# First block's opening: modulation products with the condition as the stationary operand on four column groups

## The reference, cut to what matters

```
c_act = jax.nn.silu(c)
for l in range(DEPTH):
    mod = c_act @ w_ada[l] + b_ada[l]                 # 1024 x 3072 weights
    shift, scale, gate = jnp.split(mod, 3, axis=-1)
    h = rms_norm(x, norm_g[l]) * (1.0 + scale[:, None]) + shift[:, None]
    proj = h @ w_in[l]
    ...
```

## Time and profile before

| | us |
|---|---|
| median of 3 runs | 2635.62 |
| lowest and highest | 2634.14, 3508.53 |
| the profiled execution: its time | 2632.88 |
| its span in the profile | 2631.1 |
| PE busy in the span | 2471.4 (94%) |
| DVE, ACT, POOL busy | 1205.1, 983.9, 631.0 |
| first product of the second stage | 94.13 after the span's start |

### The profile page before, as it was taken

The page is one execution under the profiler, slowest core; times in us unless marked ns, Lnnn a source line. Parts: engine busy times, 40 slices in busy tenths (PEclk is TensorE's granted clock), DMA queues, the critical chain, the costliest instruction groups (busy, mean ns, idle before and its releaser), DMA issues. The chain is left out here.

```text
span 2631.1 us, 33028 instructions
## 1 busy us (share of the span) xinstructions
PE 2471.4 (94%) x13180; PEld 2023.3 (77%) x13180; DVE 1205.1 (46%) x1668; ACT 983.9 (37%) x2095; POOL 631.0 (24%) x292
## 2 busy tenths in 40 slices
PE   6999999898998999887999999999999999999998
PEld 6877787676877777776878887667788888888886
DVE  3493402683562520485562265550653333333336
ACT  3223423573522432375342444553622121212123
POOL 2211121132321122032231121212323323232331
PEclk9999999898998999898999998999999999999999
DMA  7242110003211211002211100003211212121213
GB/s 215 64 136 89 41 52 30 33 1 113 80 47 66 73 33 48 17 17 97 72 57 43 53 1 5 21 9 120 96 32 48 65 32 65 32 65 33 64 35 150
DMA packets 139182, 154.56 MB, mean 59 GB/s; under 512 B 7436, under 2 KB 109203, under 8 KB 139029
## 3 DMA queue, kind: packets, MB, share of 16 engines
q1 hardware_dynamic: 136096, 152.05, 17.8%
q10 hardware_dynamic: 2933, 0.39, 0.1%
HBM read 135.65 MB, written 16.78 MB: 58 GB/s over the span
## 5 line engine op out<-in xcount | busy, mean ns | idle before, releaser
L665 PE MATMUL ps<-hT_hi,w_hi 128*128 128x512 f32 x1088 | 426.0, 392 | 14.7 <-DVE hT_lo L3389 5.8
L665 PE MATMUL ps<-hT_lo,w_hi 128*128 128x512 f32 x1088 | 425.0, 391 | 0.0
L665 PE MATMUL ps<-hT_hi,w_lo 128*128 128x512 f32 x1088 | 424.7, 390 | 0.0
L665 PEld LDWEIGHTS ps<-hT_hi,w_hi 128*128 128x128 f32 x1088 | 205.3, 189 | 59.2 <-issue 16.3
L665 PEld LDWEIGHTS ps<-hT_hi,w_lo 128*128 128x128 f32 x1088 | 205.2, 189 | 42.8
L665 PEld LDWEIGHTS ps<-hT_lo,w_hi 128*128 128x128 f32 x1088 | 205.3, 189 | 42.3
L601 POOL TENSOR_TENSOR w_lo<-ffn_raw,w_hi 128x2048 fp32r<-128x2048 f32 (+1 forms) x32 | 164.1, 5127 | 111.5 <-ACT w_hi L575 111.5
L3643 DVE TENSOR_SCALAR work<-work,fcols 128x1024 f32<-128x1024 f32 x44 | 33.2, 755 | 287.3 <-ACT work L3600 287.3
L3600 ACT ACTIVATE work<-ps 128x512 f32<-128x512 f32 x88 | 52.3, 596 | 278.4 <-PE ps L665 271.7
L575 ACT ACTIVATE w_hi<-ffn_raw 128x2048 fp32r<-128x2048 f32 (+1 forms) x32 | 59.6, 1864 | 248.4 <-PE ps L665 155.6
L3624 POOL TENSOR_TENSOR ffn_hid_lo<-work,ffn_hid_hi 128x1024 fp32r<-128x1024 f32 x22 | 64.9, 2949 | 346.8 <-ACT ffn_hid_hi L3614 346.8
(11 more groups left out here) (493 smaller groups left out, 5417.5 us busy)
## 6 DMA issues: line engine op xcount, KB each, us to landing
ffn_raw<-in_ffn_w_up SPq DMA_DIRECT2D x40, 512.0 KB, 5.2
mix_gla<-in_w_ada SPq DMA_DIRECT2D x32, 512.0 KB, 3.6
xres<-big SPq DMA_DIRECT2D x24, 512.0 KB, 2.6
difp_raw<-in_w_in SPq DMA_DIRECT2D x10, 1024.0 KB, 5.2
ffn_raw<-in_ffn_w_down SPq DMA_DIRECT2D x10, 1024.0 KB, 5.0
open_ada<-in_w_ada SPq DMA_DIRECT2D x16, 512.0 KB, 7.0
gla_wraw<-in_w_in SPq DMA_DIRECT2D x8, 1024.0 KB, 5.8
big<-xres SPq DMA_DIRECT2D x2, 4096.0 KB, 16.1
```

The source lines that it names most:

```text
L665: mm = nc.tensor.matmul(out, l, r, start=(job.part != 1 and c == 0 and k == 0), stop=(job.evac and c == job.chunks - 1 and k == 2))
```

## The change

The modulation is now made for pairs `p` of chunks (256 channels), four in all, with the operands exchanged: the column `cact[:, j]`, repeated 32 times, is the stationary operand (128 rows x 32 columns), and the weights (128 x 256) move. Of the eight blocks `j` of 128 inputs, block `j` goes to column group `j % 4`, which is PSUM partitions `32 (j % 4)` to `32 (j % 4) + 31`, and to bank `j // 4`. Nothing is accumulated: each of the 8 results has its own place. ACT copies bank 0 to `open_part`, DVE adds bank 1 (`rows`), and the row thus made has on each of 128 partitions a sum of two blocks, in four groups of 32 equal rows. `columns(p)` then multiplies the row's four 128x128 pieces (stationary) by a column of 1/32 (`open_share`), which adds the groups and turns the row to four columns in bank 7. `gains(p)` makes two chunks at once.

Tiles of `w_ada` are now 128x8x256 (1 MB, in runs of 1 KB), 8 in all, in a ring of 4; `open_wraw` comes after tile 3. `lam.dots` comes after the first four scalings on DVE, two copies of `r` on ACT go, and `later.turn` moves to the end and to bank 0.

```diff
-        ada, f, wraw = sb("ada", [P, 8, KC, P]), sb("f", [P, 4, 512]), sb("wraw", [P, KC * WCOLS])
+        ada, f, wraw = sb("ada", [P, 4, KC, WCOLS]), sb("f", [P, 4, 512]), sb("wraw", [P, KC * WCOLS])
+        part_a, row, share = sb("part", [P, 512]), sb("row", [P, 512]), sb("share", [P, 1])
...
-        later = Columns(nc, ctx, m, "bcols", groups, extra, bank=7)
+        later = Columns(nc, ctx, m, "bcols", groups, extra, bank=0)
...
-        TILES, UNITS, RING = 2 * KC, 2 * KC, 5
+        PAIRS, UNITS, RING = KC // 2, 2 * KC, 5
+        GROUPS, OUT = 4, 448
...
-            for t in range(TILES):
-                if t >= 8:
-                    sp.wait_ge(s_mod, (t - 8) // 2 + 1)
-                col = D * (t % 2) + P * (t // 2)
-                sp.dma_start(ada[:, t % 8, :, :], wtile(a["w_ada"][0], col, P)).then_inc(s_ada[t % 8], 16)
-                if t == 5:
+            for t in range(2 * PAIRS):
+                if t >= 4:
+                    sp.wait_ge(s_mod, t // 2 - 1)
+                sp.dma_start(ada[:, t % 4, :, :], wtile(a["w_ada"][0], D * (t % 2) + WCOLS * (t // 2), WCOLS)).then_inc(
+                    s_ada[t % 4], 16)
+                if t == 3:
                     load_tile(sp, wraw, job, s_wraw)
...
-            def modulation(c):
-
-                if c >= 2:
-                    pe.wait_ge(s_gain, c - 1)
+            def modulation(p):
+
+
+                if p:
+                    pe.wait_ge(s_part, p)
+                    pe.wait_ge(s_row, p)
                 for k in range(2):
-                    t = 2 * c + k
-                    pe.wait_ge(s_ada[t % 8], 16 * (t // 8 + 1))
+                    t = 2 * p + k
+                    pe.wait_ge(s_ada[t % 4], 16 * (t // 4 + 1))
                     for j in range(KC):
-                        mm = nc.tensor.matmul(m.ps[:, c % 2, k:k + 1], ada[:, t % 8, j, :], m.cact[:, j:j + 1],
-                                              start=(j == 0), stop=(j == KC - 1))
+                        g = 32 * (j % GROUPS)
+                        mm = nc.tensor.matmul(m.ps[g:g + 32, j // GROUPS, WCOLS * k:WCOLS * k + WCOLS],
+                                              m.cact[:, j:j + 1].to_broadcast([P, 32]), ada[:, t % 4, j, :],
+                                              start=True, stop=True)
                 mm.then_inc(s_mod, 1)
+
+            def columns(p):
+
+                pe.wait_ge(s_row, p + 1)
+                if p:
+                    pe.wait_ge(s_gain, p)
+                else:
+                    pe.wait_ge(s_share, 1)
+                    cols.wait_cols(pe)
+                for k in range(4):
+                    mm = nc.tensor.matmul(m.ps[:, 7, OUT + 4 * p + k:OUT + 4 * p + k + 1], row[:, P * k:P * k + P],
+                                          share[:, :], start=True, stop=True)
+                mm.then_inc(s_col, 1)
...
-            modulation(0)
-            for c in range(1, KC):
-                modulation(c)
-                turn(2 * c - 2)
-                turn(2 * c - 1)
-                if c == KC - 2:
-                    cols.wait_cols(pe)
-                    later.turn(pe)
-            turn(UNITS - 2)
-            turn(UNITS - 1)
+            for p in range(PAIRS):
+                modulation(p)
+                between = 2 if p else 0
+                for u in range(4 * p, 4 * p + between):
+                    turn(u)
+                columns(p)
+                for u in range(4 * p + between, 4 * p + 4):
+                    turn(u)
+            later.turn(pe)
...
-                own.mark(nc.scalar.activation(r[:, a:b], r[:, a:b], ACT.Exp, scale=-0.5))
-                own.settle()
+                nc.scalar.activation(r[:, a:b], r[:, a:b], ACT.Exp, scale=-0.5).then_inc(s_r, 1)
+
+            def partial(p):
+                act.wait_ge(s_mod, p + 1)
+                if p:
+                    act.wait_ge(s_row, p)
+                nc.scalar.activation(part_a[:, :], m.ps[:, 0, :], ACT.Copy).then_inc(s_part, 1)
...
-            nc.scalar.activation(r[:, 0:4], r[:, 0:4], ACT.Copy).then_inc(s_r, 1)
...
             for u in range(UNITS):
                 c = u // 2
+                if u % 4 == 0:
+                    partial(u // 4)
                 act.wait_ge(s_turned, u + 1)
-                act.wait_ge(s_gain, c + 1)
+                act.wait_ge(s_gain, u // 4 + 1)
...
-            def gains(c):
-
-                col, ps = m.cols[:, 0, :], m.ps[:, c % 2, 0:2]
-                dve.wait_ge(s_mod, c + 1)
-                own.mark(nc.vector.tensor_tensor(m.shift[:, 0, c:c + 1], ps[:, 0:1],
-                                                 col[:, m.C_BADA + c:m.C_BADA + c + 1], ALU.add))
-                own.mark(nc.vector.tensor_tensor(m.gain[:, 0, c:c + 1], ps[:, 1:2],
-                                                 col[:, m.C_BADA + KC + c:m.C_BADA + KC + c + 1], ALU.add))
+            def rows(p):
+
+                dve.wait_ge(s_part, p + 1)
+                if p:
+                    dve.wait_ge(s_col, p)
+                nc.vector.tensor_tensor(row[:, :], m.ps[:, 1, :], part_a[:, :], ALU.add).then_inc(s_row, 1)
+
+            def gains(p):
+
+                col, both = m.cols[:, 0, :], slice(2 * p, 2 * p + 2)
+                mod = m.ps[:, 7, OUT + 4 * p:OUT + 4 * p + 4]
+                dve.wait_ge(s_col, p + 1)
+                own.mark(nc.vector.tensor_tensor(m.shift[:, 0, both], mod[:, 0:2],
+                                                 col[:, m.C_BADA + 2 * p:m.C_BADA + 2 * p + 2], ALU.add))
+                own.mark(nc.vector.tensor_tensor(m.gain[:, 0, both], mod[:, 2:4],
+                                                 col[:, m.C_BADA + KC + 2 * p:m.C_BADA + KC + 2 * p + 2], ALU.add))
                 own.settle()
-                nc.vector.scalar_tensor_tensor(out=m.gain[:, 0, c:c + 1], in0=m.gain[:, 0, c:c + 1], scalar=1.0,
-                                               in1=col[:, m.C_NORM + c:m.C_NORM + c + 1], op0=ALU.add,
+                nc.vector.scalar_tensor_tensor(out=m.gain[:, 0, both], in0=m.gain[:, 0, both], scalar=1.0,
+                                               in1=col[:, m.C_NORM + 2 * p:m.C_NORM + 2 * p + 2], op0=ALU.add,
...
-            lam.dots(dve)
             for i in range(NT // 2):
                 scaled(i)
+            lam.dots(dve)
...
-            gains(0)
-            for c in range(1, KC):
-                gains(c)
-                high_and_low(2 * c - 2)
-                high_and_low(2 * c - 1)
-            high_and_low(UNITS - 2)
-            high_and_low(UNITS - 1)
+            for p in range(PAIRS):
+                rows(p)
+                gains(p)
+                for u in range(4 * p, 4 * p + 4):
+                    high_and_low(u)
```

More of the change, by code:

```diff
@@ L262, in stage_open @@
     with ExitStack() as ctx:
[L263 to L267, removed]
+        (s_x0, s_x1, s_c, s_pos, s_t, s_cact, s_act, s_r, s_xn, s_ada0, s_ada1, s_ada2, s_ada3, s_mod, s_part,
+         s_row, s_col, s_gain, s_own, s_turned, s_f, s_hi, s_lov, s_lop, s_wraw, s_whi, s_wlo, s_share) = semaphores(
+            nc, ctx, m, "open", "x0 x1 c pos t cact act r xn ada0 ada1 ada2 ada3 mod part row col gain own turned f hi "
+            "lov lop wraw whi wlo share")
+        s_ada = (s_ada0, s_ada1, s_ada2, s_ada3)
         def sb(name, shape, dt=F32):
@@ L332, in _ @@
             const.identity(pool)
+            pool.memset(share[:, :], 1.0 / 32).then_inc(s_share, 1)
             cols.zero(pool)
@@ L416, in _ @@
             roots(1)
-            nc.scalar.activation(r[:, 4:8], r[:, 4:8], ACT.Copy).then_inc(s_r, 1)
             lam.exp(act)
```

## The result

Median after 2605.2 us (2603.11 to 2606.94, 4 runs), before 2634.88 (4 runs). The ratio is 0.9892, 95% interval 0.9872 to 0.9911: 1.1% less, inside the 2% that count as no change here. The profiled execution took 2604.45 us, its span is 2602.7, against 2632.88 and 2631.1. (One execution of the kernel before, 3508.53, lies far off all others; without it the median before is 2634.14.)

What follows compares the result with a forecast made beforehand. PE, loading 128 fp32 weight columns per one-column product, bounds the opening: eight chunks of 8.4 us. Pairs of 3.4 + 3.5 + 1.75 = 8.65 us, then the tail, give 27.7 us less: 2608 us, range 2599 to 2621.

Steps and rivals of the forecast that it cites:

- The sum: Opening at the lower clock: pair 1 turned at 43.1, pair 2 at 52.2, next stage at 66.4, 27.7 us less.
- the signs: Opening: pair 1's records within 3.4 to 3.8 us; a columns product waiting over 1 us for DVE would refute.
- The clock: PE in the opening: lower clock, chance 0.43, 2608 us; higher for part or all, 0.27, 2600 to 2605.
- The rival's sum: Opening at 2.4 GHz, weights the bound: next stage at 59.7, 34.4 us less, 2601; clock higher for part or all, 0.27.
- The copy to `w_hi`: ACT's 1.90 us copy after unit 5 delays unit 7; pair 2's bank copy comes 0.4 us after its cover ends.
- The factor of four groups: Modulation products: four column groups give factor 4, 3.4 us a pair; factor 2 to 3 had chance 0.18, 2611 to 2620.
- The switches between tilings: PE between column groups and full width: 0.2 us at most each, eight switches, 1.6 us, left to the range.
- Pair 0: First pair: products end 27.7, row 29.2, columns 31.0, turns 34.5; 1.5 us hand-off exposed.
- The weights: w_ada loads in 1 KB runs: 3.1 us a tile, tile 0 at 22.9, tile 7 at 49.0.
- The loss at 28 to 30: Weight transfers: only 168 GB/s moved at 28 to 30, 1.3 us lost, not removed by the change.
- The tail: From the last gains to the next stage's first product: 7.64 us less 0.45, taken as 7.2.
- The serial rival: Column groups take turns: 18.9 us a pair, 11.8 us slower, 2647; chance 0.05.

Runs made afterwards that it cites:

- experiment 1: Changed kernel with POOL's subtraction left out, w_lo filled with zeros (part of the computation missing): 2594.22 us, next stage's first product at 60.17.
- experiment 7: Changed kernel with the subtraction for w_lo moved from POOL to DVE, behind unit 7: 2601.61 us, ratio to before 0.9882.
- experiment 4: Changed kernel with sums accumulated in PSUM, DVE alone copying, and one column group in place of four: 2613.03 us, ratio to before 0.9923.
- Experiment 6: Kernel before with only the loads changed, to 1 MB tiles in runs of 1 KB: 2633.25 us, ratio to before 1.0005.
- experiment 5: Changed kernel with each w_ada tile loaded by two transfers in runs of 512 B: 2606.42 us, ratio to before 0.9901.
- 3: Changed kernel with blocks j and j + 4 accumulated in one PSUM bank, DVE alone copying it, ACT's copy gone: 2601.27 us, ratio to before 0.9878.
- 11: Changed kernel run again unedited on another chip, source of the second profile: 2605.47 us, ratio to before 0.9891.
- experiment 2: Changed kernel with POOL's subtraction in four pieces of 512 columns, ahead of its units 7, 9, 11, 13: 2604.73 us, ratio to before 0.9889.
- 9: Changed kernel with sums in PSUM, subtraction in two halves on DVE, next pair's row copied ahead of a pair's last unit: 2597.84 us, ratio to before 0.9866.
- 10: Changed kernel with PSUM sums, subtraction halves on DVE, early row copy, and all low parts on DVE: 2601.78 us, ratio to before 0.9878.
- experiment 8: Changed kernel with sums accumulated in PSUM, DVE alone copying, and POOL's subtraction in four pieces: 2600.32 us, ratio to before 0.988.

## Why the prediction was right, and where not

The time: 2605.2 for 2608, inside the range. The sum gave 27.7 us less for the opening, 28.1 came. That agreement is luck in part. **Two steps were wrong and cancelled each other**: pair 1 was done 2.75 us ahead of the sum (40.35 for 43.1), pair 3's products began 1.8 us behind it (54.00 for 52.2), and pair 3, at the higher clock for the most part, gave that back (gains at 59.21 for 59.2). Two of the signs that I had named came true: pair 1's records took 1.93 us, not 3.4 to 3.8, and a columns product waited over 1 us for DVE (5.77).

**The clock (wrong).** I gave the lower clock 0.43 and its rise 0.27. It rose near 35.0, ahead of pair 1 (within pair 1 in the second profile). Products, turns and columns of pair 1 then take half, those of pair 3 nearly so. My reason against it was a row of the attention at 0.50 with PE busy 7.87 of 10 us; it didn't carry over. The rival's sum, 59.7, lies near what experiment 1 finds with the collision gone (60.17), but not by its path: tile 7 was never waited for there, PE waited 2.78 us for pair 2's row, and pair 3's products ran at the lower clock.

**The copy to `w_hi` (mis-sized).** "Pair 2's copy comes 0.4 us after its cover has ended" was 5.77 us and 7.08 in the second profile. Experiment 1 splits the 5.77: 3.73 us are POOL's subtraction, the first user of `w_hi`, which holds DVE's CAST of unit 6; some 2 are units 6 and 7 on DVE and ACT behind the 1.90 us copy, under turns that at the higher clock cover 1.09 us, not 1.75. I followed only ACT's queue. ACT's copy of bank 0 was made at 45.64; the row was added at 49.66. Before, the same subtraction stood in the trace, held a DVE instruction and cost nothing. Timeline of the kernel before:

```profile
56.93 4.51 POOL L340 TENSOR_TENSOR w_lo<-open_wraw,w_hi 128x2048 fp32r<-128x2048 f32 x1
...
60.57 0.16 DVE L446 TENSOR_TENSOR shift<-ps,cols 128x1 f32<-128x1 f32 x1 [5.05 <-PE ps L355]
...
60.83 0.63 DVE L451 SCALAR_TENSOR_TENSOR gain<-gain,cols 128x1 f32<-128x1 f32 x1
...
89.82 1.26 POOL L313 TENSOR_TENSOR hT_lo<-open_f,hT_hi 128x512 fp32r<-128x512 f32 x1 [7.80 <-DVE hT_hi L457]
89.96 1.41 DVE L457 CAST hT_hi<-open_f 128x512 fp32r<-128x512 f32 x1 [0.21 <-ACT open_f L426]
```

The gain on one column takes 0.63 us in place of 0.16 and ends at 61.46, with the subtraction (61.44). L446, which reads PSUM, isn't held. DVE had idled 5.05 us, so nobody felt it. At 89.96 even the CAST itself takes 1.41 us for 0.43, beside POOL's low part. I had not read these rows; they were the sign. The Trainium skill (SBUF — State Buffer, Who interferes with whom) has the rule: VectorE in a two-port mode, or with two inputs in SBUF, and a reading GpSimd exclude each other for the whole instruction. The trace agrees, for the CAST (4.16), the gains (0.63) and the other way round (POOL's 3.24 in experiment 7).

**The factor of four groups (right)**, at both clocks; experiment 4 has the same products on one group. What hangs on it is less than I wrote: not the whole gain, but some 8 of 29 us, as experiment 4 shows. The Trainium skill (TensorE: Matmul & The Clock Gate, Part 3: Packing small matmuls) gives 2.38 for three column tiles; this trace shows no such loss with four. The switches between tilings cost 0.1 us at most, for the 0.2 that I had as a bound: turns begun at 31.48 at 0.217 each end at 34.95, and the products start at 35.06.

**Pair 0 (right).** Row, columns and turns were to be done at 29.2, 31.0 and 34.5; they were at 29.7, 31.6 and 35.0, late by some 0.5 us; tile 1, from which the sum goes, came 0.37 us late (26.37 for 26.0), the first tile 0.55 (23.45 for 22.9). The hand-off was 1.44 us for 1.5, and 0.42 and 0.43 us in pairs 1 and 3, where I had under 0.5.

**The weights (right but for the end).** They ran at 350 GB/s, 3.0 us a tile for 3.1, and all were there by 48, in time for pair 3. The loss at 28 to 30 was smaller (288 GB/s for 168). Experiment 6 shows that the runs alone give nothing; experiment 5 that they give 2 to 3 us once PE is quick, more than the 1 us that I had at the lower clock.

**The tail (right).** 66.05 - 59.21 = 6.84 us for 7.2.

**The serial rival (wrong price).** 2647 held the lower clock fixed. One group gives 2613, still faster than before; its 13.7 us a pair became 7.09 with the clock up, and the long products cover the waits.

## What to carry to other kernels

A sum that adds up is no proof: go through it step by step in the new trace, and look where it was right for the wrong reason. When an engine stops being the bound, search the old trace for short instructions of the other engines that took several times their usual length beside something else; they were free, and can become the next stall. And for work on PE made denser, carry the sum at both clock levels down to the end, with each cover shortened as well, and not as a rival with a price of its own.

## What the hardware showed that I hadn't expected

- POOL's subtraction of 128x2048 held a DVE CAST for 3.7 us (4.16 for 0.43), in every profile in which they met (4.25, 4.25, 4.19 and 4.16 in experiments 3, 4, 5 and 11). DVE operations that read PSUM ran through beside POOL (0.68 us at 49.66 after, 0.16 at 60.57 before). In pieces the hold spreads over several DVE instructions (experiment 2).
- The clock rose in the opening with all these forms, and fell again around pair 2 in most. The length of PE's wait there doesn't decide it alone: it fell with 5.77 us (changed kernel), 2.78 (experiment 1), 1.73 (9) and 1.54 (10), among others, and stayed up with 2.01 (8) and with 1.68 between long products (4). In experiment 8 it fell after the next wait, 3.52 us.
- Four column groups of fp32 over all 128 rows, each with 256 moving columns, run fully side by side: 16 products (32 records) in 1.93 us at the higher clock.
